# Attention steps by odd and even pairs: where the maximum, the scaling, the stores of y and the weight halves stand

## The reference

```python
keys = jnp.concatenate([k_meta, kn], axis=1)      # 16 meta keys, then this and the previous block of 128
scores = einsum('bqhgd,bkhd->bhgqk', qn, keys) - slopes * dist
scores = jnp.where(valid, scores, -jnp.inf)
m = jnp.maximum(jnp.max(scores, axis=-1, keepdims=True), sink)
p = jnp.exp(scores - m)
probs = p / (jnp.sum(p, axis=-1, keepdims=True) + jnp.exp(sink - m))
out = einsum('bhgqk,bkhd->bqhgd', probs, vals)
```

## Time and profile before

| what | us |
|---|---|
| median of 3 runs | 1621.34 (1620.97 to 1622.37) |
| the profiled execution's own time | 1623.07 |
| its span in the trace | 1621.3 |
| attention loop in the trace | about 495 to 731 |
| PE, DVE, ACT, POOL busy in those 236 us | 225.34, 183.52, 172.96, 192.91 |

### The profile page before, as it was taken

One profiled execution on the slowest core, in us unless ns is written; L12 is line 12 of the kernel. 1 busy time (PEld: TensorE's weight loads), 2 busy tenths in 40 slices (PEclk: granted clock), 3 DMA queues, 4 the chain that ended last, 5 costly groups with the idle time before them and its releaser, 6 DMA issues.

```text
span 1621.3 us, 22775 instructions
## 1 busy us (share of the span) xinstructions
PE 1603.1 (99%) x7942; PEld 1335.2 (82%) x7942; DVE 1062.5 (66%) x2063; ACT 781.8 (48%) x1615; POOL 406.4 (25%) x584
## 2 busy tenths in 40 slices
PE   9999999999999999999999999999999999999999
PEld 7888888888888787878888888888888888888887
DVE  7984556666566778766564438876666656766675
ACT  6733244455456778772222126655555544444442
POOL 0111011121135888874221000121111222100000
PEclk9999999999999999999999999999999999999999
DMA  8533323265344575667553223354444389733452
GB/s 296 180 102 117 111 104 104 97 215 207 136 154 135 160 182 149 178 163 244 168 197 113 72 66 117 121 178 156 150 143 145 121 306 365 244 98 98 148 183 92
DMA packets 132113, 255.95 MB, mean 158 GB/s; under 512 B 15024, under 2 KB 52320, under 8 KB 132000
## 3 DMA queue, kind: packets, MB, share of 16 engines
q1 hardware_dynamic: 88304, 135.89, 26.4%
q0 software_dynamic: 43408, 118.48, 22.3%
q10 hardware_dynamic: 288, 0.14, 0.0%
HBM read 159.67 MB, written 69.47 MB: 141 GB/s over the span
## 4 chain that ended last, share of the span: by engine, by line
PE 93%; POOL 2%; DVE 2%; DMA 1%; ACT 1%; issue 1%; DVEq 0%; ACTq 0%
PE bank L1226 29%; PE bank L1231 29%; PE bank L1230 29%; POOL PR L1102 2%; PE bank L1529 1%; PE bank L1561 1%; PE bank L1543 1%; DMA PW<-PR 1%; POOL RT L1118 1%; PE bank L1269 0%; PE bank L1661 0%; PE bank L1445 0%; PE bank L1611 0%; DVE WL L2412 0%; PE bank L1578 0%
## 5 line engine op out<-in xcount | busy, mean ns | idle before, releaser
L1226 PE MATMUL bank<-WH,ADH 128*128 128x512 f32 x448 | 174.3, 389 | 0.0
L1230 PE MATMUL bank<-WH,ADL 128*128 128x512 f32 x448 | 174.3, 389 | 0.0
L1231 PE MATMUL bank<-WL,ADH 128*128 128x512 f32 x448 | 174.3, 389 | 0.0
L1102 POOL TENSOR_SCALAR PR<-PR,RC 128x272 f32<-128x272 f32 (+1 forms) x128 | 142.9, 1349 | 36.7 <-DVE RC L2978 36.7
L2338 ACT CAST ADH<-ARAW 128x512 fp32r<-128x512 f32 x112 | 69.6, 621 | 170.9 <-PE bank L1231 156.8
L3234 DVE TENSOR_TENSOR ADL<-ARAW,ADH 128x512 fp32r<-128x512 f32 x112 | 77.5, 692 | 97.0 <-ACT ADH L2338 97.0
L1226 PE MATMUL bank<-HN,WH 128*128 128x512 f32 x344 | 138.0, 401 | 0.0
L1231 PE MATMUL bank<-HN,WH 128*128 128x512 f32 x344 | 135.9, 395 | 0.0
L1230 PE MATMUL bank<-HN,WL 128*128 128x512 f32 x344 | 135.7, 394 | 0.0
L1226 PE MATMUL bank<-SOPH,WH 128*128 128x512 f32 x256 | 99.8, 390 | 0.0
L1231 PE MATMUL bank<-SOPL,WH 128*128 128x512 f32 x256 | 99.6, 389 | 0.0
(11 more groups left out here) (392 smaller groups left out, 4327.2 us busy)
## 6 DMA issues: line engine op xcount, KB each, us to landing
ARAW<-uop SPq DMA_DIRECT2D x112, 256.0 KB, 3.4
uop<-US POOLq DMA_DIRECT2D x64, 256.0 KB, 2.9
WRAW<-in_w_up SPq DMA_DIRECT2D x15, 1024.0 KB, 6.2
PW<-PR SPq DMA_DIRECT2D x56, 272.0 KB, 2.6
RAW<-in_w_in SPq DMA_DIRECT2D x52, 256.0 KB, 4.4
uop<-UA POOLq DMA_DIRECT2D x48, 256.0 KB, 3.2
proj<-SA POOLq DMA_DIRECT2D x36, 256.0 KB, 2.3
RT<-proj POOLq DMA_DIRECT2D x8, 1024.0 KB, 7.2
```

Of the source, the lines that this page charges most:

```text
L1102: pr = pool.tensor_scalar(keys, keys, RC[:, b, hl:hl + 1], None, ALU.mult)
L1226: mm = pe.matmul(bank, ahi, bhi, start=first, stop=False, skip_group_check=onto)
L1230: pe.matmul(bank, alo, bhi, start=False, stop=False, skip_group_check=onto)
L1231: return pe.matmul(bank, ahi, blo, start=False, stop=last, skip_group_check=onto)
```

## The change

Five things move; no operation is added or removed.

1. `new_slabs` takes the eight halves of slabs 4 and 5 from the table `SPLIT_AT`. Half k of the next slab is made in the step T that holds gate step 57, 58, 60, 61, 63, 64, 66 or 68 (counted from the start of the slab in use, so 64 is step 0 of the next slab). In steps T: for slab 4, halves 0 to 7 were made in T = 9, 9, 10, 10, 10, 11, 11, 12 and are made in T = 9, 10, 10, 11, 12, 12, 13, 14; for slab 5 in T = 37, 37, 37, 38, 38, 39, 39, 40, now 37, 37, 38, 39, 40, 40, 41, 42.
2. DVE in even steps: `lo_p` of pair T-3, then `top(T)`, then `lo_meta`. In odd steps the order of these stays.
3. DVE in odd steps: `inverse(T)` directly behind, ahead of the next block's work, the gates and the halves.
4. ACT in odd steps: `take_p`, `take_next_q`, `weigh(T)`, then `take_y` and the rest.
5. POOL: y of group G is added in step 2G + 8, behind the scaling of the odd pair and ahead of a load of KV or DT, instead of in step 2G + 7, behind the scaling of the even pair.

```diff
+SPLIT_AT = (57, 58, 60, 61, 63, 64, 66, 68)
...
-        if 56 <= k < 60 or k >= 60 and slab + 1 < SLAB_E:
+        if slab > SLAB_D and k + 64 in SPLIT_AT:
+            out.append((slab, SPLIT_AT.index(k + 64)))
+        if slab + 1 < SLAB_E:
+            if k in SPLIT_AT:
+                out.append((slab + 1, SPLIT_AT.index(k)))
+        elif 56 <= k < 60:
             out.append((slab + 1, k - 56))
...
+                if T >= LAG + 5 and T % 2 == 0:
+                    G = (T - LAG - 5) // 2
+                    pool.wait_ge(yc_done[G % 2], 32 * (G // 2 + 1) + (16 if G % 2 else PL0))
+                    for par in range(2):
+                        pool.dma_start(y_place(G, par), y_part(G, 1, par), accum_op=ALU.add)\
...
-                if T >= LAG + 2 and T % 2 == 1:
-                    take_y((T - LAG - 2) // 2)
+                if T % 2 == 1:
+                    if T in NEXT_Q:
+                        take_next_q(*NEXT_Q[T])
+                    if T < NPAIR:
+                        weigh(T)
+                    if T >= LAG + 2:
+                        take_y((T - LAG - 2) // 2)
...
-                if T < NPAIR:
+                if T < NPAIR and T % 2 == 1:
                     top(T)
                 if LAG <= T < NPAIR + LAG:
                     lo_p(T - LAG)
+                if T < NPAIR and T % 2 == 0:
+                    top(T)
+                if LAG <= T < NPAIR + LAG:
+                    lo_meta(T - LAG)
...
+                if T < NPAIR and T % 2 == 1:
+                    inverse(T)
```

More of the change, by code:

```diff
@@ L1095, in _ @@
             load_sq(NB - 1)
-            for T in range(STEPS + 2):
+            for T in range(STEPS + 4):
                 if 1 <= T <= NPAIR:
@@ L1104, in _ @@
                     pr.then_inc(pn_rdy, 1)
+                if T >= LAG + 5 and T % 2 == 0:
[3 more added lines that the diff above has]
+                        pool.dma_start(y_place(G, par), y_part(G, 1, par), accum_op=ALU.add)\
+                            .then_inc(yf_done[G % 2], 16)
                 if T % 8 == 1 and 2 <= T // 8 + 1 < NB:
@@ L1113, in _ @@
                     load_kv(n + NKV)
[L1114 to L1119, removed]
             pool.wait_ge(gst_done[0], 16 * (8 + NAHEAD // 2))
@@ L2191, in _ @@
                     hi_v(T // 8 + 1).then_inc(qh_rdy, 1)
-                if T in NEXT_Q:
+                if T in NEXT_Q and T % 2 == 0:
                     take_next_q(*NEXT_Q[T])
@@ L2201, in _ @@
                 splits = new_slabs(T) if T <= NPAIR + 1 else []
-                for slab, k in splits[:2]:
+                for slab, k in splits[:1]:
                     split_hi(slab, k)
-                if T < NPAIR:
+                if T < NPAIR and T % 2 == 0:
                     weigh(T)
-                for slab, k in splits[2:]:
+                for slab, k in splits[1:]:
                     split_hi(slab, k)
@@ L2950, in lo_p @@
             def lo_p(pair):
-                n, G = pair // 8, pair // 2
+                n = pair // 8
                 dve.wait_ge(ph_rdy, split_of(pair))
@@ L2954, in lo_p, with lo_meta @@
                    .then_inc(pl_rdy, 1)
+            def lo_meta(pair):
+                G = pair // 2
                 if pair % 2 == 1:
@@ L3014, in _ @@
                     split_lo(slab, k)
-                if T < NPAIR and not (T % 8 == 0 and T // 8 + 1 < NB):
+                if T < NPAIR and T % 2 == 0 and not (T % 8 == 0 and T // 8 + 1 < NB):
                     inverse(T)
```

## The result

The changed kernel takes **1641.17 us** (median of 4 runs, 1640.64 to 1643.36), the kernel before 1621.15 us (4 runs, 1620.91 to 1622.37). The ratio is 1.0124, 95% interval 1.0107 to 1.0142: 20 us slower, where 3.3 were forecast and 1630 was the end of the range.

What follows compares the result with a forecast made beforehand. PE was taken to bound the kernel, busy for 99% of the span. Terms 3.0 + 0.3 − 1.5 + 0.3 + 1.7 − 0.5 = +3.3 us on a median of 1621.34 gave 1624.6 us; range 1617.5 to 1630.

Steps and rivals of the forecast that it cites:

- The weight halves: Gate steps in steps 15 and 43: PE waits 2.1 and 3.2 us for half 7; net +0.3 and +3.0 us.
- The clock: PE: one stretch at half clock behind the long waits of steps 15 and 43, +1.7 us, bounds 0 and +3.4.
- Y's landing: ACT, odd steps: y lands about 9.1 us behind the odd scores, `take_y` asks at 8.5, so ACT waits some 0.6.
- rival 3: Odd steps: y landing 9.5 us behind the odd scores delays cast, low part, maximum, meta rows; 1631 us; chance 0.13.
- `take_y` behind the weighing: ACT, odd steps: `take_y` after `weigh` frees its buffer later; no term of its own, taken from the low part's gain.
- Low part ahead of the maximum: DVE, even steps: low part of P done about 0.7 us earlier, shortening waits of `values`: −1.5 us, bounds 0 and −4.3.
- Odd pairs first: Weigh and reciprocal of odd pairs 0.3 to 1 us earlier, even pairs later: net +0.3 us, bounds −0.9 and +3.
- The last pair: End of loop: scaling 0.3 us earlier, fewer transfers ahead of copy: −0.5 us, −3.6 if wait and half clock go.
- rival 2: Last pair's copy lands in 2.6 us, removing its wait of 1.9 and half clock of 1.7: about 1617.9; chance 0.12.

Runs made afterwards that it cites:

- run 3: The kernel before with the new table of weight halves and nothing else of the change: 1626.11 us, ratio 1.0031.
- run 1: The changed kernel with the old table of weight halves: 1633.34 us, ratio 1.0078.
- run 6: The changed kernel with the last half of a slab made with gate step 67 in place of 68: 1633.97 us, ratio 1.0083.
- run 7: The changed kernel with `take_y` and SyncE's store of y's first half one step later, for all but the last four groups: 1628.58 us, ratio 1.0048.
- run 2: The changed kernel with y added ahead of the odd scaling on POOL again, as before: 1634.03 us, ratio 1.0077.
- run 4: The kernel before with y's adding moved behind the odd scaling on POOL, nothing else: 1676.50 us, ratio 1.0341.
- run 5: The changed kernel with the old table and y added in its old place, so only the orders are left: 1626.69 us, ratio 1.0038.
- run 13: The changed kernel with old table, y added in its old place, and `take_y` ahead of the weighing again in odd steps: 1623.77 us, ratio 1.0009.
- run 15: As run 14, with the maximum ahead of the low part of P in even steps again: 1622.42 us, ratio 1.0002 against the kernel before.
- run 14: The changed kernel, last half with gate step 67, `take_y` and SyncE's store a step later for all groups but the last: 1619.05 us, ratio 0.9982.
- run 8: The kernel before with only the low part of P ahead of the maximum in even steps: 1621.98 us, ratio 1.0006.
- run 11: The changed kernel, last half with gate step 67, `take_y` and store a step later, y added ahead of the odd scaling again: 1652.23 us.
- 10: The changed kernel, last half with gate step 67, `take_y` and SyncE's store a step later for all but the last four groups: 1622.11 us.

## Why the prediction was wrong

**The weight halves: mechanism and places right, size right alone and short in company.** The forecast was 3.2 us of wait in step 43 and 2.1 in step 15. The trace has 3.51 and 1.71 for half 7, and beside them 0.66 and 1.20 for half 6, which DVE makes a step earlier and which the forecast left at nothing. It took +3.0 + 0.3, with one half clock 5.0; the table alone costs 5.0 (run 3). In the changed kernel it costs 7.5 (run 1). Step 15 waits in both, 1.9 us in run 3 and 2.9 here. What the changed kernel lacks is the gain of steps 9 to 14 that pays for it in run 3: 2.5 us there, 0.2 here (its lateness goes from 2.4 us to 2.2). The forecast had 2.5 of it stay and added the orders as a term of their own; no run separates why it is gone in their company.

**The clock: one half clock was counted, two came**, both behind the waits for half 7. By the prediction's way of counting they cost 3.5 and 1.7 us (0.77 and 0.88, 0.91 and 0.92 in the windows), and the two of before, 1.7 each, are gone. The net of 1.8 is near the forecast's +1.7 by luck, since that counted one new one. Both vanish in run 6 with the long waits, and the wait of 1.21 us left in step 15 was not followed by one there. A wait of 1.71 us in step 15 was followed by half clock in the changed kernel and not in run 7. Before, a wait of 2.1 us passed without and two of 1.8 and 1.9 did not. No run here tells what decides between such cases.

**Y's landing: this step failed.** The wait itself was foretold: ACT's was to rise from 1.0 to over 8 us, and it is 11.0. What failed is its price. The prediction let ACT wait "some 0.6 in most odd steps", put the cast of P late by 0 to 1 us behind it, and charged nothing beyond keeping −1.5 of the low part's gain. Y's place costs 7.6 us instead (run 2), because a late `take_y` makes the cast of P, the low part and `values` late in turn, as the rows from 680.53 on show. The mechanism stood there as rival 3, which "binds" if y lands 9.5 us behind the odd scores, priced at 6.5 us above the forecast: its price was nearly right and its chance of 0.13 too low. The estimate had put y's landing at 9.1, and by the timelines of the changed kernel the median of 28 groups is 9.1. But the single ones go from 7.9 to 11.0, and 8 of them are past 9.5. A median said nothing of these. That the median came out is in part luck: the scaling ends after 3.9 us and not 4.3, and the landing takes 4.3 and not 3.8. That `take_y` can be a link of a ring was not seen; run 4, where turns of some 9 us set the pace of the loop, shows it.

By "DMA: Bandwidth & Descriptors" in the Trainium skill (anatomy of one DMA) a 64 KB transfer was an estimate of 2.2 us, and ACT would not have waited. The runs disagree: 4.45 us in the chain of run 4, 4.12 here, and ACT waits 11.0 us.

**`take_y` behind the weighing was costed at nothing: the second failed step.** The text says that "its buffer frees later", and prices only the landing. But the place costs 4.7 us with y's adding where it was (run 5 against 13). The prediction followed what is queued behind the waiting adding on POOL, and not what is queued behind the newly waiting weighing on ACT. That weighing waits for the maximum 35.0 us in all, 56 times (the same view of the kernel before has 5.7, 4 times), though by most of it not because of this place: run 13, with `take_y` ahead again, still has 26.8 us in 32. The buffer, y's bank, is not what bound: in the traces of these runs no late `values` waited for it.

**Low part ahead of the maximum: −1.5 with bounds 0 and −4.3** holds at both ends. Alone it is within what can be told (1.0 slower, −0.3 to 2.4); with the other waits cured it brings 3.4 us (run 15 less run 14). One step of its reasoning is wrong: "the meta rows' low part comes as before". In the median of the even steps it is ready 2.9 us behind the start of the step's transposes before, 3.4 in run 8 and 3.3 in run 14, since DVE now sits idle for the cast of P ahead of it, and the meta matmuls of `values` wait for it in some 20 places (9.4 us in weight loads in run 8, 11.2 in the changed kernel). In the changed kernel the low part of P itself gains nothing over the kernel before (2.4 us behind that start, before 2.5, in run 8 1.9): y's landing holds the cast.

**Odd pairs first (+0.3):** the trace has no transposes held by the copy in steps 20, 28, 36 and 44. In the loop they are held by it at 506.33 (0.41), at 533.10 (1.23), and for pairs 61 and 63 at the end. The sign wasn't isolated. The room was larger than estimated: the scaling of a pair was taken as 2.6 us from the earlier trace rows, and is 1.9 by the reading below.

**The last pair (−0.5):** the drift shrinks by 1.0 us there. Its copy lands after 3.75 us against 4.84, 0.83 of wait is left of 1.86, and the clock stays at 1.00. Against this `values` waits 1.75 us behind it.

The range was to reach down to rival 2, which is 1617.9 in one place and 1617.5 in the other; nothing hangs on the difference.

So the loss is: last half one step too late 6.6 of the table's 7.5, y behind the odd scaling 7.6, `take_y` behind the weighing 4.7, other orders about 1.5. With the whole 7.5 they sum to 21.3. What stays open is the 1.2 us by which the parts exceed the whole, which the intervals of the runs cover, the path by which the place of `take_y` costs its 4.7, the 1.5 us of the other orders, and what holds the clock.

## What to carry to other kernels

Where an operation is moved to behind a wait, follow the ring: what it releases, what that releases, and whether this comes back to it. The length of the ring against the length of a step says whether it binds, and a margin of 0.4 us between a median landing and the point where it binds is none when single landings spread over 3 us. Edits on a chain of several queues are no sum: y's edit costs 55 us alone, 8 with all orders and the table, and leaving it out costs 29 once `take_y` is late (run 11 against 10), so test each edit in the company that it would have. Where a table spreads preparation, look at the last piece, which comes last in its engine's queue. Here it was made in the step just ahead of its use, and one number that put it a step earlier was worth 6.6 us.

## What was not expected of the hardware

POOL's scaling of a pair appears with two durations, about 1.9 us and about 2.6 us. The timeline of POOL in run 4:

```profile
605.58 1.90 POOL L1103 TENSOR_SCALAR PR<-PR,RC 128x272 f32<-128x272 f32 x2 [3.15 <-DVE RC L2982]
607.43 2.00 POOL L1110 DMA_DIRECT2D RT<-YA  x2
608.68 2.31 POOL L1047 DMA_DIRECT2D KV<-proj  x2
610.28 2.66 POOL L1103 TENSOR_SCALAR PR<-PR,RC 128x272 f32<-128x272 f32 x2
```

The one of 2.66 starts at 610.28, 0.7 us before the issue ahead of it ends (608.68 + 2.31 = 610.99). Behind that end it takes 1.95. So the listed start of a scaling behind a DMA issue can lie inside the issue, and from its end on the scaling takes 1.9 us like any other. This fits the group's mean, 1349 ns before and 1026 after: 26 of the 64 pairs' scalings are listed from inside an issue before, 7 after. By this reading the prediction's 2.6 us was time of the issue. The other reading, that the scaling starts there and is slowed until the issue ends, gives the same rows; no run tells them apart, and what POOL is held for is the same in both.
